# The second mixer's scan preparation between its input products: step sizes feature-major and early, blocks from last to first

## What is computed

```python
h = modulate(x, sh1, sc1)
proj = h @ w_in[layer]                       # 256 x (256 + 768 + 1792 + 12)
u, z, xbc, dt_raw = jnp.split(proj, split_at, axis=-1)
...
xbc = jax.nn.silu(causal_depthwise_conv(xbc, conv_w, conv_b))
xs, bm, cm = jnp.split(xbc, [SSD_WIDTH, SSD_WIDTH + G * N], axis=-1)
dt = jax.nn.softplus(dt_raw + dt_bias)       # step sizes: 12 heads
a = -jnp.exp(a_log)
y = ssd_scan(xh, dt, a, bm, cm) + xh * d_skip
```

## Time and profile before

| | us |
|---|---|
| median of 3 runs | 1129.49 |
| lowest and highest run | 1128.2, 1129.98 |
| span of the profiled execution, first to last instruction | 1124.6 |
| PE busy in the span | 1053.0 (94%) |
| VectorE, ScalarE, GpSimd busy | 461.9, 354.3, 39.6 |

### The profile page before, as it was taken

One profiled execution on the slowest core, in us unless ns is written; L12 is line 12 of the kernel. 1 busy time (PEld: TensorE's weight loads), 2 busy tenths in 40 slices (PEclk: granted clock), 3 DMA queues, 4 the chain that ended last, 5 costly groups with the idle time before them and its releaser, 6 DMA issues.

```text
span 1124.6 us, 17911 instructions
## 1 busy us (share of the span) xinstructions
PE 1053.0 (94%) x7545; PEld 717.5 (64%) x7545; DVE 461.9 (41%) x698; ACT 354.3 (32%) x508; POOL 39.6 (4%) x32
## 2 busy tenths in 40 slices
PE   5999999999999999999999999999899989898986
PEld 5996777899699999877986453444244333242432
DVE  4784244467554453556657351222122212121212
ACT  5752322454463443355543220111011111010102
POOL 0002200002001010000000000000000000000000
PEclk9999999999999999999989999999999999999999
DMA  9454378335726556454366869999999999999994
GB/s 327 153 204 159 109 243 256 108 150 177 230 88 218 156 182 224 169 205 163 133 225 240 337 278 422 421 421 422 422 421 422 422 422 422 422 422 422 422 422 191
DMA packets 95445, 316.36 MB, mean 281 GB/s; under 512 B 8262, under 2 KB 33174, under 8 KB 70678
## 3 DMA queue, kind: packets, MB, share of 16 engines
q1 hardware_dynamic: 94342, 312.75, 72.4%
q10 hardware_dynamic: 1040, 2.69, 0.7%
HBM read 314.37 MB, written 1.05 MB: 280 GB/s over the span
## 4 chain that ended last, share of the span: by engine, by line
PE 72%; DMA 21%; DVE 4%; ACT 2%; issue 1%; SPq 0%; POOL 0%; DVEq 0%; ACTq 0%
DMA arena<-in_w 20%; PE bank L1480 12%; PE bank L769 11%; PE bank L771 11%; PE bank L770 11%; PE bank L1504 4%; PE bank L755 4%; PE bank L1027 3%; PE bank L942 2%; PE bank L1460 1%; PE bank L976 1%; PE bank L746 1%; PE bank L1517 1%; PE bank L716 1%; PE bank L728 1%
## 5 line engine op out<-in xcount | busy, mean ns | idle before, releaser
L1480 PE MATMUL bank<-ring,hT 128*64 128x512 f32 x512 | 226.6, 594 | 28.6 <-DMA arena<-in_w 27.5
L1480 PE MATMUL bank<-arena,hT 128*64 128x512 f32 x512 | 226.7, 595 | 0.0
L771 PE MATMUL bank<-h_high,ring_low 128*128 128x256 f32 x688 | 192.8, 280 | 0.0
L1480 PEld LDWEIGHTS bank<-ring,hT 128*64 128x64 f32 x512 | 67.9, 137 | 180.4 <-issue 130.7
L560 DVE TENSOR_TENSOR ring_low<-ring,hi_high 128x2048 fp32r<-128x2048 f32 (+2 forms) x58 | 126.0, 2218 | 100.8 <-ACT hi_high L1651 100.7
L769 PE MATMUL bank<-h_high,hi_high 128*128 128x256 f32 x528 | 147.8, 280 | 0.0
L770 PE MATMUL bank<-h_low,hi_high 128*128 128x256 f32 x528 | 147.2, 279 | 0.0
L1651 ACT ACTIVATE hi_high<-ring 128x2048 fp32r<-128x2048 f32 (+2 forms) x58 | 104.5, 1852 | 91.3 <-DMA ring<-in_w_ffn_up 33.5
L771 PEld LDWEIGHTS bank<-h_high,ring_low 128*128 128x128 f32 x688 | 129.9, 189 | 0.0
L1504 PE MATMUL bank<-arena 128*64 128x512 f32 x384 | 113.3, 595 | 7.1 <-DVE hT L2778 6.6
L2784 DVE TENSOR_TENSOR arena<-arena,bank 128x512 f32<-128x512 f32 x16 | 17.3, 1083 | 229.2 <-ACT arena L2008 229.2
(11 more groups left out here) (399 smaller groups left out, 1702.4 us busy)
## 6 DMA issues: line engine op xcount, KB each, us to landing
arena<-in_w SPq DMA_DIRECT2D x112, 1024.0 KB, 22.7
ring<-in_w SPq DMA_DIRECT2D x80, 1024.0 KB, 20.3
ring<-in_w_in SPq DMA_DIRECT2D x12, 2048.0 KB, 7.8
ring<-in_w_ada SPq DMA_DIRECT2D x7, 2048.0 KB, 8.2
ring<-in_w_ffn_gate SPq DMA_DIRECT2D x11, 1024.0 KB, 5.4
ring<-in_w_ffn_up SPq DMA_DIRECT2D x11, 1024.0 KB, 7.9
ring<-in_w_ada SPq DMA_DIRECT2D x20, 512.0 KB, 5.2
ring<-in_w_ffn_down SPq DMA_DIRECT2D x5, 2048.0 KB, 7.9
```

Source lines behind the costliest of these rows:

```text
L771: return mm(ps, a[1], b[0], start=False, stop=stop)
L1480: last = mm(both(6 + half, x), hg[:, k, (2 * q + x) * CAP:(2 * q + x + 1) * CAP], w13s[x][k // 4][:, k % 4, half * EF:(half + 1) * EF], st ...
```

## The change

- The chunks of `w_in_2` are loaded in the order 0, 1, 5, 4, 3, 2, and the blocks are multiplied from 6 to 0.
- The step sizes are computed first and feature-major: 24 products of 256 columns, with the 128 columns of chunk 5 that end in the twelve as the stationary side. ScalarE copies the 128 x 256 result to `dtrow`, and PE turns it back in two transposes (`dtt`).
- What needs the step sizes or single blocks stands between the blocks: `dtt` after block 5, pooling, running sums and the first chunk's `rb` after block 4, the second chunk's `rb` after block 3, `cb` after block 2, the transposes of block 2 after block 1. The rest follows block 0.
- On ScalarE the softplus stands between blocks 5 and 4, the decays' exponentials between blocks 2 and 1, and each silu behind the copy of the next block or later. VectorE follows the same order.
- Of the last two chunks GpSimd subtracts the second half (semaphore `in2_pool`), VectorE the first.
- `ada_chunk(8)` stands behind the first `mt` transposes, not before them. Some buffers move to other places.

```diff
-    o += [("xb", mm) for mm in range(7)]
-    o += [("dt2",), ("pl",), ("ad", 6), ("cs",), ("pm",)]
-    o += [("rb", i, q) for i in range(NT) for q in range(3)]
-    o += [("cb", i) for i in range(NT)]
-    o += [("xt", i, a) for i in range(NT) for a in range(2)] + [("bt",), ("as", 6), ("ad", 7)]
+    o += [("dt2",), ("xb", 6), ("xb", 5), ("dtt",), ("xb", 4), ("pl",), ("cs",)]
+    o += [("rb", 0, q) for q in range(3)] + [("xb", 3)] + [("rb", 1, q) for q in range(3)] + [("xb", 2)]
+    o += [("cb", i) for i in range(NT)] + [("xb", 1)] + [("xt", i, 1) for i in range(NT)] + [("xb", 0)]
+    o += [("ad", 6), ("pm",), ("bt",), ("as", 6)] + [("xt", i, 0) for i in range(NT)] + [("ad", 7)]
...
+IN2 = (0, 1, 5, 4, 3, 2)
+XB_ORDER = (6, 5, 4, 3, 2, 1, 0)
+DT_AT = 2 * P + SH - P
...
-        for c in range(6):
+        for c in IN2:
             stream(("in2", c), [(0, cols(w_in2, c * 512, min(c * 512 + 512, w_in2.shape[1])))],
-                   ("uz", 1, c) if c < 2 else ("xb", 2 * c - 3) if c < 5 else ("dt2",))
+                   ("uz", 1, c) if c < 2 else ("xb", 2 * c - 4))
...
-                    pe.wait_ge(S("in2_low"), 2 * (n - BY_TWO) + 2)
+                    pos = n - BY_TWO
+                    pe.wait_ge(S("in2_low"), 2 * pos + 2 if pos < 4 else pos + 5)
+                    if pos >= 4:
+                        pe.wait_ge(S("in2_pool"), pos - 3)
...
+            def dt_rows():
+
+                halved(("in2", 5))
+                w = parts_view(("in2", 5), "p (k c) -> p k c", k=KD)
+                ps = write(pe, ("dt2",))
+                for k in range(KD):
+                    last = by_parts(ps[:, 0:SEQ], [x[:, k, DT_AT:DT_AT + P] for x in w], (hT_hi[2][:, k, :], hT_lo[:, k, :]),
+                                    k == 0, k == KD - 1)
+                last.then_inc(*full(("dt2",)))
...
+            dt_rows()
+            xb(6)
+            xb(5)
+            drained(pe, ("dt2",))
+            transposes(("dtt",), [(i, dtrow[:, i * P:(i + 1) * P]) for i in range(NT)])
+            xb(4)
+            pooled()
+            decay_sums()
+            decay_rows(0)
+            xb(3)
+            decay_rows(1)
+            xb(2)
+            pe.wait_ge(S("xs"), 4)
             for i in range(NT):
-                for k in range(KD):
-                    last = by_parts(ps[:, i * 16:i * 16 + SH], [x[:, k, i * P:(i + 1) * P] for x in (hT_hi[2], hT_lo)],
-                                    [x[:, k, 256:256 + SH] for x in w], k == 0, k == KD - 1)
-            last.then_inc(*full(("dt2",)))
-
-            pe.wait_ge(S("pool_in"), 16 * 5)
+                gram(i)
+            xb(1)
+            pe.wait_ge(S("xs"), 5)
             for i in range(NT):
-                drained(pe, ("uz", i, 0))
-            ps = write(pe, ("pl",))
-            for g in range(GRP):
-                o, c0 = 64 * (g % 2), SEQ * (g // 2)
+                x_tokens(i, 1)
+            xb(0)
             ada_chunk(6)
...
+            transposes(("bt",), [(g, xs[:, 6 + g, 0:P]) for g in range(GRP)])
+            ada_sum(6)
             pe.wait_ge(S("xs"), 7)
             for i in range(NT):
-                ps = write(pe, ("cb", i))
-                for g in range(GRP):
-                    t = slice(i * P, (i + 1) * P)
-                    last = mm(ps[:, g * P:(g + 1) * P], xs[:, 6 + g, t], xs[:, 10 + g, t], start=True, stop=True)
-                last.then_inc(*full(("cb", i)))
-
-            def transposes(key, pairs):
-                ps = write(pe, key)
-                for c, src in pairs:
-                    last = nc.tensor.transpose(ps[:, c * P:(c + 1) * P], src, ident)
-                last.then_inc(*full(key))
-
-            for i in range(NT):
-                for a in range(2):
-                    transposes(("xt", i, a), [(c, xs[:, 4 * a + c, i * P:(i + 1) * P]) for c in range(4 if a == 0 else 2)])
-            transposes(("bt",), [(g, xs[:, 6 + g, 0:P]) for g in range(GRP)])
+                x_tokens(i, 0)
...
             ada_sum(7)
-            ada_chunk(8)
             for i in range(NT):
                 pe.wait_ge(S("ys"), i + 1)
                 for a in range(2):
                     transposes(("mt", i, a), [(c, ys[:, i, (4 * a + c) * P:(4 * a + c + 1) * P])
                                               for c in range(4 if a == 0 else 2)])
                 if i == 0:
+                    ada_chunk(8)
...
+            ps = filled(act, ("dt2",))
+            A_(dtrow, ps[:, 0:SEQ], ACT.Copy).then_inc(*free(("dt2",)))
+            raw(6)
+            raw(5)
             act.wait_ge(S("par2_in"), 16 * 3)
             act.wait_ge(S("dt_abs"), 1)
             A_(alog, alog, ACT.Exp).then_inc(S("alog"), 1)
             A_(dtmp, dtmp, ACT.Exp, scale=-1.0).then_inc(S("dt_e"), 1)
             act.wait_ge(S("dt_e"), 1)
             A_(dtmp, dtmp, ACT.Ln, bias=1.0).then_inc(S("dt_ln"), 1)
-            ada_rows(6)
+            raw(4)
+            silu_of(0)
+            high_parts(BY_TWO + 5)
+            silu_of(1)
+            raw(3)
+            silu_of(2)
+            raw(2)
+            silu_of(3)
             drained(act, ("cs",))
             A_(ea[:, 0, 0:SH], acs[:, 1, 0:SH], ACT.Exp)
             A_(ea[:, 1, 0:SH], acs[:, 2, 0:SH], ACT.Exp).then_inc(S("ea"), 1)
+            for i in range(NT):
+                for q in range(3):
+                    drained(act, ("rb", i, q))
+                A_(dec[:, i], dec[:, i], ACT.Exp).then_inc(S("dec_e"), 1)
+            raw(1)
+            silu_of(4)
+            for i in range(NT):
+                tokens_out(i, 1)
+            raw(0)
+            silu_of(5)
+            silu_of(6)
+            ada_rows(6)
             ps = filled(act, ("pm",))
             for h in range(2):
                 ins = A_(mixT[:, h, :], ps[:, h * SEQ:(h + 1) * SEQ], ACT.Copy, scale=par("pool_scale_2", h))
             ins.then_inc(*free(("pm",)))
-            for i in range(NT):
-                for q in range(3):
-                    drained(act, ("rb", i, q))
-                A_(dec[:, i], dec[:, i], ACT.Exp).then_inc(S("dec_e"), 1)
-            for i in range(NT):
-                for a in range(2):
-                    ps = filled(act, ("xt", i, a))
-                    w = 512 if a == 0 else 256
-                    A_(xtok[:, i, 512 * a:512 * a + w], ps[:, 0:w], ACT.Copy).then_inc(*free(("xt", i, a)))
             ps = filled(act, ("bt",))
             A_(btk, ps[:, :], ACT.Copy).then_inc(*free(("bt",)))
+            for i in range(NT):
+                tokens_out(i, 0)
...
+            for n in (BY_TWO + 4, BY_TWO + 5):
+                _, words = split_words(n)
+                pool.wait_ge(S("high"), 2 * n + 2)
+                low_part(nc.gpsimd, n, words // 2, words).then_inc(S("in2_pool"), 1)
...
+            conv(6)
+            first_half_low(BY_TWO + 4)
+            dve.wait_ge(S("router_in"), 64)
+            ps = filled(dve, ("dtt",))
+            V.tensor_tensor(dtr, ps[:, 0:2 * P].rearrange("p (i c) -> p i c", i=NT)[:, :, P - SH:P], cast(dtb.unsqueeze(1), P, NT, SH),
+                            ALU.add).then_inc(*free(("dtt",)))
+            drained(dve, ("dtt",))
+            V.scalar_tensor_tensor(dtmp, dtr, -1.0, dtr, ALU.mult, ALU.max).then_inc(S("dt_abs"), 1)
+            conv(5)
+            dve.wait_ge(S("dt_ln"), 1)
+            link(V.scalar_tensor_tensor(dtr, dtr, 0.0, dtmp, ALU.max, ALU.add))
+            dve.wait_ge(S("alog"), 1)
+            V.scalar_tensor_tensor(da, dtr, -1.0, cast(alog.unsqueeze(1), P, NT, SH), ALU.mult, ALU.mult).then_inc(S("da"), 1)
+            conv(4)
+            ps = filled(dve, ("pl",))
+            V.tensor_copy(dif.rearrange("p a b -> p (a b)"), ps[:, :]).then_inc(*free(("pl",)))
+            ps = filled(dve, ("cs",))
+            V.tensor_copy(acs[:, :, 0:SH], ps[:, 0:48].rearrange("p (i c) -> p i c", i=3)[:, :, 0:SH]).then_inc(*free(("cs",)))
+            drained(dve, ("cs",))
+            decays(0)
+            conv(3)
+            first_half_low(BY_TWO + 5)
+            decays(1)
+            conv(2)
             for i in range(NT):
                 ps = filled(dve, ("cb", i))
                 V.tensor_tensor(cbm[:, i], heads4(ps), cast(K("causal").unsqueeze(1), P, GRP, P), ALU.mult).then_inc(*free(("cb", i)))
+            for i in range(NT):
                 dve.wait_ge(S("dec_e"), i + 1)
                 drained(dve, ("cb", i))
                 d4 = dec[:, i].rearrange("p (g r) t -> p g r t", g=GRP)
                 V.tensor_tensor(d4, d4, cast(cbm[:, i].unsqueeze(2), P, GRP, SR, P), ALU.mult).then_inc(S("dec"), 1)
-                dve.wait_ge(S("ea"), 1)
+            conv(1)
+            conv(0)
+            dve.wait_ge(S("ea"), 1)
```

131 lines of the change are left out of this document (70 added, 61 removed), and 6 rows, old and new, of the table PLACED.

## The result

The change made the kernel slower: 1143.68 us (median of 4 runs, 1141.9 to 1145.49) against 1129.74 us (the kernel before, now the median of four runs), a ratio of 1.0129 with a 95% interval of 1.011 to 1.0148. The forecast was 1139.3, its range ended at 1142.5: the sign was right, the size too small, and the time lies 1.2 us outside the range.

What follows compares the result with a forecast made beforehand. PE's work and waits between first block product and first `mx` were taken as the bound. Waits of 14.0 against 7.2 us (+6.8) plus 3.0 of clock falls lengthen the span 1124.6 to 1134.4; with 4.9, 1139.3 us, range 1133.5 to 1142.5.

Steps and rivals of the forecast that it cites:

- break-even of 7.2 us: PE before `mx`: 5.6 us of work saved plus 1.6 us of existing waits; the kernel loses if new waits exceed it.
- The five waits: PE before `cs`, `cb`, block 2's `xt`, `ada_rows(6)` and `ada_rows(8)`: 4.0, 2.3, 3.6, 2.8 and 1.3 us.
- wait 1: PE before `cs`, waiting for the step sizes: 4.0 us, with GpSimd's low part holding VectorE's taps of block 6.
- the rival that GpSimd holds nobody: Before `cs`: VectorE's taps not held, wait 1.2 us, time 1135.0 or 1133.5 us; chance 0.18.
- The work: PE before `mx`: saves 3.5 us on `dt2`, 1.4 on pooling, 0.65 on `ada_chunk(6)`; 5.6 us in all.
- Waits 1 and 3: PE before `cs` (4.0 us) and block 2's `xt` (3.6 us): one clock fall behind each, 3.0 us together.
- the gap at 306.57: Earlier stretch of 2.33 us with PE busy for 0.45, followed by low clock; the yardstick for counting falls.
- waits 2 and 4: PE before `cb` (2.3 us, silu of block 3) and `ada_rows(6)` (2.8 us, modulation's copy); no clock fall counted.
- one more fall an upper bound: Behind the 2.3 us wait before `cb` and the 2.8 us one before `ada_rows(6)`: at most one fall together.
- The rival of closed waits: ScalarE behind blocks 2, 1 and 0: copies and silus finish under PE's work, 4.7 us faster, 1124.8 us; chance 0.07.
- the distance from the first `mx` to the end changes by no more than 1 us: First output product to kernel end: length unchanged; a change over 1 us would make the prediction wrong.
- With the 4.9 us around it: Whole run: time outside the span, added to the forecast span of 1134.4 us to give 1139.3.

Runs made afterwards that it cites:

- Experiment 2: Changed kernel with the silus of blocks 3 and 4 moved ahead of the copies of blocks 2 and 1 on ScalarE: 1133.23 us.
- experiment 7: Changed kernel with GpSimd out of the low parts and the step sizes right behind block 6's taps on VectorE: 1138.8 us.
- experiment 8: Changed kernel with silus before copies, step sizes first on VectorE, no GpSimd in low parts, modulation's copy before the last silu: 1124.75 us.
- experiment 9: Changed kernel with GpSimd's half of the first of the two low parts starting only once VectorE has written `da`: 1139.86 us.
- experiment 3: Changed kernel with GpSimd taken out of the low parts, VectorE subtracting both halves: 1139.64 us.
- experiment 10: Changed kernel with all reorderings together, and `ada_chunk(8)` and its copy put back ahead of the `mt` transposes: 1125.43 us, ratio 0.995 to the kernel before.
- Experiment 5: Kernel before with only the step sizes changed, to 24 products of 256 columns and two transposes: ratio 0.9984 to the kernel before.
- experiment 4: Kernel before with GpSimd subtracting the second halves of the last two chunks' low parts: ratio 1.0015 to the kernel before.
- experiment 11: Kernel before with the wide step sizes, and two thrown-away products in PE's wait ahead of the running sums: ratio 0.9972 to the kernel before.
- experiment 12: Kernel of all reorderings with `ada_chunk(8)` put back, plus one thrown-away product in each of two pauses before `mx`: ratio 0.9965 to the kernel before.
- experiment 1: Changed kernel with PE multiplying thrown-away products in its five waits of the stretch: 1134.4 us.
- experiment 6: Changed kernel with the silus of blocks 3 and 4 before the copies, and its three remaining waits filled with thrown-away products: 1129.15 us.

## Why the prediction was right and where it failed

**The sign and the mechanism: right.** Against a break-even of 7.2 us of waits there are 12.6. The five waits stood where the order put them and were released by what the forecast named. Experiment 2 takes two of them away, experiment 7 another and experiment 8 all but 2.1 us, and the time follows, down to faster than before.

**The waits: 14.0 forecast, 12.6 measured, 1.4 too many.** Half of that is wait 1, 3.28 for 4.0. Its GpSimd part was right to the tenth, 2.8 (experiment 9), though it rested on one row of 0.3 us; the rival that GpSimd holds nobody, given 0.18, falls. The other part is that PE came 0.4 us later to it (at 553.2, 21.8 us after the first block product, where I had 21.4) and the sums 0.4 earlier. The hold is paid by wait 1, as I had it. Whether the kernel would be faster without GpSimd is another question: VectorE's own second half takes almost the same place in wait 1, and the ratios of the changed kernel and experiment 3 have intervals that just meet, at 1.011.

**The work: 72.65 at full clock forecast, 73.5 measured** (experiments 8 and 10, which have no fall in the stretch), so 0.9 too little. Experiment 5 saves 78.25 - 74.69 = 3.6, with a fall of 1.6 in it, so 5.2 of the 5.55 that I had put down for `dt2`, pooling and modulation. The other 0.5 lies among the interleaved pieces and wasn't traced.

**The clock: this is the step that failed.** "Waits 1 and 3 are longer than the gap at 306.57, so I count a fall behind each, 2 x 1.5 = 3.0 us." There were four, one behind each wait of 2.1 us or more in this kernel, and PE's busy time shows 80.05 - 73.54 = **6.5 us**, 1.6 each. The size of one fall was right. The number was read from a single gap, taken as a bound where it was only an instance, and by its length: of its 2.33 us PE was busy for 0.45, so it was idle for 1.9 at most. By that row waits 2 and 4, forecast at 2.3 and 2.8 us, were longer as well, and wait 4 was longer than even the 2.33. I called them "about as long" and put them at nothing; measured at 2.12 and 2.47, they brought a fall each. I had called one more fall an upper bound and never priced a fourth. With all three corrections the account of the stretch closes: 89.6 + 0.9 - 1.4 + 3.5 = 92.6. That is 3.0 of the 4.4 us between 1139.3 and 1143.68. Of the rest, 0.25 is the median of the kernel before, which moved, and some 1.1 lies outside the stretch: two of the four runs, 1144.6 and 1145.49, have a mean clock of 0.988 where the profiled one, 1142.76, has 0.990, and where they lost it no trace shows. A certain number of falls isn't shown to follow from the waits either: experiment 7 has the same wait 2 and no fall behind it. What the rows supported was a range from two falls to four.

**The rival of closed waits** was right in its mechanism, and its place: ScalarE behind blocks 2, 1 and 0. It didn't happen by itself, the order of the calls has to be changed for it (experiments 2 and 8).

**That the distance from the first `mx` to the end changes by no more than 1 us** held, 516.5 and 516.6, but partly by chance: both kernels have one fall there, in different places. Over all profiled executions that length is 514.8 to 515.1 with no fall, 516.5 to 516.9 with one, 518.1 with two.

**"With the 4.9 us around it"** was wrong. A run's time is about 2.0 us above its own span (1142.76 and 1140.7; 1124.10 and 1122.2 in experiment 8). With 2.0 us around it, the span of 1124.6 belongs to an execution of about 1126.6 us, shorter than the median, and the sum stood on the median, so the forecast was not shifted by it.

## What to carry to other kernels

Where an engine takes its instructions in order and pieces of work are put between one another, ask for each wait which short instruction ends it and what stands before that one on its own engine; here two exchanged pairs of calls were worth 8.6 us of the stretch, and with GpSimd left out as well, such exchanges turned 1.3% slower into 0.3% faster. Price every wait of TensorE over about 2 us twice, by itself and by the fall of the clock that may follow it, 1.6 us here, and take the number of falls, not the mean clock, as the quantity to forecast and to range over. A pause that is filled, or work that is saved ahead of a late chain, pays only if no fall and no wait comes next: look one stage on before counting the gain.

## What the runs showed of the hardware

- **GpSimd stops one VectorE instruction for as long as its own lasts.** The last of the six taps in experiment 9 starts at 557.0, just behind GpSimd's instruction of 556.94, and takes 4807 ns where the median is 483; GpSimd ends at 561.56. The other hold of that row is the same with GpSimd's 550.49 to 555.01. The forecast had this from one row of 1.40 us; four holds of 2.8 to 4.3 us now bear it out (the changed kernel, experiment 4, and two in experiment 9). In experiment 4 a VectorE subtraction that started first held GpSimd for about 2 us, and the taps behind it were held in turn, 12 in 7.55 us where 12 took 5.31 elsewhere in that kernel. The Trainium skill (SBUF — State Buffer, SBUF: two separate sides) says that the one that starts first has the port pair for the whole instruction; these rows agree.
- **A wait of a given length doesn't settle whether the clock falls.** 2.12 us brought a fall in the changed kernel and none in experiment 7. Waits of 1.1 to 1.2 us were followed by no fall within 10 us in any profiled execution. Pauses of 0.4 and 0.5 us ahead of `mx` went with a fall there in the kernel before and in experiments 4, 10 and 11, and with none in experiment 5, where the pauses are the same (0.37 and 0.49).
- **A fall that is avoided may come later.** In the profiled executions of experiments 11 and 12 one fall was gone and another stood further on; those of experiments 1 and 6, where all longer waits were filled, had none from 528 us to 665 us. The executions of one kernel differ among themselves, though (mean clock 0.993 to 0.999 in experiment 6), so that the filling moved those falls is not shown, and what decides where they come these runs don't settle.
- **The unchanged part scatters.** The first block product starts between 528.1 and 534.1 us in the fourteen profiled executions, behind PE products that are the same in all. The five with no fall of the clock ahead of it start at 528.1 to 530.2, the seven with one fall at 528.3 to 532.5, and the two with two falls or one of double length at 533.6 and 534.1, so falls are a part of the scatter and not all of it. The 3.2 us by which the changed kernel's stretch starts later in its profile are of this kind, so that the medians, 13.9 us apart, and the stretch, 12.8, tell the same story and the spans, 16.1 apart, overstate it.
